# Bias rows repeated from a DRAM row, forget rows loaded behind the first weights, later sums at the second gate tile

## The reference, cut to what matters

```python
def dilated_bias(rel_bias, g):                       # mixer B: one bias row per group and head
    r = B_DILATIONS[g]
    n_slots = B_WINDOWS[g] // r + 1
    b = rel_bias[t5_bucket(jnp.arange(n_slots, dtype=jnp.int32) * r)]
    return b[:, g * B_HPG:(g + 1) * B_HPG].T.astype(jnp.float32)
...
    # mixer A, sample tokens: forget values come by page from a pool, then a cumulated sum
    logf = jnp.concatenate(
        [logf_pool[page_table].reshape(DB, P, H).astype(jnp.float32), logf_new], axis=1)
    cT = jnp.cumsum(logf, axis=1).transpose(0, 2, 1)
    s = jnp.einsum("nqhd,nkhd->nhqk", q, k).astype(jnp.float32) * ATTN_SCALE
    s = s + cT[:, :, P:, None] - cT[:, :, None, :]
...
    h = rmsnorm(x, g_pre)
    qa, ka, va, fa, za, qb, kb, vb, zb, ga, gb = jnp.split(h @ w_in, cuts, axis=-1)
    u_a = (o_a.reshape(N, L, A_WIDTH) * jax.nn.silu(za)) @ w_br_a
    u_b = (o_b.reshape(N, L, B_OUT_WIDTH) * jax.nn.silu(zb)) @ w_br_b
    x = x + rmsnorm((sigmoid(ga) * u_a + sigmoid(gb) * u_b) @ w_out, g_post)
```

## Time and profile before

| | |
|---|---|
| runs | 790.59, 792.75, 792.93 us (median 792.75) |
| span of the profiled execution | 790.7 us; no other time of that execution is given |
| PE busy | 650.9 us (82%) |
| DVE, ACT, POOL busy | 358.0, 248.3, 181.0 us |
| chain that ended last | PE 64%, SP's queue 16%, DVE 7%, DMA 4%, POOL 3% |
| SP's queue in that chain | L406 8%, L407 4% |
| DMA queues | q1 71.77 MB, q0 27.68 MB |

### The profile page before, as it was taken

How to read it: one execution, slowest core, us unless ns; L and a number is a source line. 1 busy time by engine, 2 the same in 40 slices (tenths; PEclk the granted TensorE clock), 3 DMA queues, 4 the chain that set the end, 5 groups by cost and what they waited for, 6 DMA issues and landing times.

```text
span 790.7 us, 12686 instructions
## 1 busy us (share of the span) xinstructions
PE 650.9 (82%) x4740; PEld 590.3 (75%) x4740; DVE 358.0 (45%) x759; ACT 248.3 (31%) x539; POOL 181.0 (23%) x203
## 2 busy tenths in 40 slices
PE   3940009999999999999998977899999989847892
PEld 3730009999899889999998977876548989837892
DVE  1820004555555544344446777432215743194662
ACT  5520012443443433343331222321112323464410
POOL 2610033011010003000034778301101221366000
PEclk9885559999999999999999999999999999987997
DMA  7199978652461433822316998735552321123111
GB/s 213 9 28 27 28 140 268 217 187 79 141 206 42 154 87 90 313 80 80 108 28 200 295 317 269 205 111 156 151 162 88 107 81 47 34 80 107 41 41 55
DMA packets 106219, 100.26 MB, mean 127 GB/s; under 512 B 6591, under 2 KB 93927, under 8 KB 105872
## 3 DMA queue, kind: packets, MB, share of 16 engines
q1 hardware_dynamic: 101936, 71.77, 31.6%
q0 software_dynamic: 4176, 27.68, 16.9%
q10 hardware_dynamic: 48, 0.01, 0.0%
HBM read 90.31 MB, written 27.96 MB: 150 GB/s over the span
## 4 chain that ended last, share of the span: by engine, by line
PE 64%; SPq 16%; DVE 7%; issue 4%; DMA 4%; POOL 3%; ACT 2%; POOLq 0%; DVEq 0%; ACTq 0%
PE pj L790 43%; SPq L406 8%; PE tr L782 4%; SPq L407 4%; PE pv L740 4%; PE pv L926 3%; DMA kv_b<-in_cache_b_kv_dram 2%; PE sc L893 2%; PE sc L901 2%; PE pv L744 2%; DVE yT L1687 1%; PE sc L790 1%; POOL prod L623 1%; PE sc L898 1%; SPq L395 1%
## 5 line engine op out<-in xcount | busy, mean ns | idle before, releaser
L790 PE MATMUL pj<-h_hi,w_hi 128*128 128x260 f32 x1088 | 323.9, 298 | 101.8 <-DVE w_lo L1315 78.6
L790 PE MATMUL pj<-h_lo,w_hi 128*128 128x260 f32 x1088 | 313.6, 288 | 0.0
L790 PE MATMUL pj<-h_hi,w_lo 128*128 128x260 f32 x1088 | 313.4, 288 | 0.0
L790 PEld LDWEIGHTS pj<-h_hi,w_hi 128*128 128x128 f32 x1088 | 211.6, 194 | 117.8 <-DVE w_lo L1315 79.0
L790 PEld LDWEIGHTS pj<-h_lo,w_hi 128*128 128x128 f32 x1088 | 211.7, 195 | 0.0
L790 PEld LDWEIGHTS pj<-h_hi,w_lo 128*128 128x128 f32 x1088 | 211.4, 194 | 0.0
L1315 DVE TENSOR_TENSOR w_lo<-w_raw,w_hi 128x1024 fp32r<-128x1024 f32 (+1 forms) x76 | 93.9, 1240 | 128.7 <-ACT w_hi L1061 128.1
L1061 ACT ACTIVATE w_hi<-w_raw 128x1024 fp32r<-128x1024 f32 (+2 forms) x84 | 81.5, 972 | 166.8 <-DMA w_raw<-in_w_in_dram 106.6
L1322 DVE COPY probT<-tr 128x256 f32<-128x256 f32 (+3 forms) x56 | 27.3, 488 | 52.9 <-PE tr L782 52.9
L623 POOL TENSOR_TENSOR prod<-kv_a,qbc 128x512 f32<-128x512 f32 x24 | 32.6, 1385 | 19.2 <-DMA kv_b<-in_cache_b_kv_dram 14.4
L926 PE MATMUL pv<-v_tok,probT 128*128 128x64 f32 x216 | 29.4, 263 | 0.0
(11 more groups left out here) (326 smaller groups left out, 961.1 us busy)
## 6 DMA issues: line engine op xcount, KB each, us to landing
w_raw<-in_w_in_dram SPq DMA_DIRECT2D x52, 512.0 KB, 5.0
kv_a<-in_cache_a_kv_dram SPq DMA_DIRECT2D x64, 256.0 KB, 3.5
out_dram<-in_cache_b_kv_dram POOLq DMA_DIRECT2D x16, 1022.0 KB, 10.0
qbc<-q_dram SPq DMA_DIRECT2D x8, 640.0 KB, 5.6
kv_b<-in_cache_b_kv_dram SPq DMA_DIRECT2D x32, 128.0 KB, 3.0
w_raw<-in_w_out_dram SPq DMA_DIRECT2D x8, 512.0 KB, 3.9
w_raw<-in_w_ple_gate_dram SPq DMA_DIRECT2D x8, 512.0 KB, 4.4
x_in<-in_x_prompt_dram SPq DMA_DIRECT2D x4, 512.0 KB, 6.5
```

What stands on the lines that cost most here:

```text
L790: ins = nc.tensor.matmul(out, w[:, k0, :], x[:, c_x, lo:hi], start=first and i == 0, stop=last and i == 2)
```

## The change

The diff has three parts.

1. **Bias rows.** `gen` goes once into a small DRAM tensor `gen_dram` (three DMAs). The 128 copies of each row are then read from that DRAM row (`bias_copies`, source of step 0) instead of from a partition of SBUF. POOL issues these 12 copies at the head of round 1, behind the stores of the forget values, and the 12 reads into `toep` (`bias_tiles`) at the head of round 2, ahead of round 2's window copies.
2. **Forget rows.** SP loads w3, w4 and w5 first. The 32 rows come eight at a time, behind the other loads of rounds 0 to 3 in SP's list. The wait for the page table stays ahead of the wait for `cum`.
3. **Later sums.** The transposes of `lf_rows` and the four products move from round 0 to behind gate tile 31 (t = 1), into a bank `tr` instead of `pv`; DVE copies `lfT` out at t = 1 and `later` at t = 2. Round 1's wait for `s_lsum` is gone; the addition of `later` waits for its copy.

The diff, cut to its core (left out: the list of semaphore names and three lines of counting):

```diff
@@ -288,6 +288,7 @@
 
         c_dram = nc.dram_tensor("c_dram", [2, AH, SEQ], F32).ap()
         toep_dram = [nc.dram_tensor(f"toep_dram{g}", [BH, P * PITCH[g]], F32).ap() for g in range(BG)]
+        gen_dram = [nc.dram_tensor(f"gen_dram{g}", [BH, PITCH[g]], F32).ap() for g in range(BG)]
         o0_dram = nc.dram_tensor("o0_dram", [SEQ, BO], F32).ap()
         m0_dram, l0_dram = (nc.dram_tensor(n, [SEQ, BH], F32).ap() for n in ("m0_dram", "l0_dram"))
         q_dram = nc.dram_tensor("q_dram", [DEC, ROUNDS * P], F32).ap()
...
@@ -401,12 +404,16 @@
             sp.dma_start(wf_raw[:, :, :], w_in[:, :, COL_F:COL_F + AH]).then_inc(s_wf, 16)
             for n in range(RING):
                 load(n)
-            sp.wait_ge(s_pt, 16)
-            for i in range(DEC * PAGES):
-                page = sp.value_load(pt[0:1, i:i + 1], min_val=0, max_val=POOL_PAGES - 1)
-                sp.dma_start(lf_rows[i:i + 1, :], A["cache_a_logf"][0, bass.ds(page, 1), :, :].rearrange("o t h -> o (t h)")).then_inc(S["s_lfr"], 16)
             for n in range(RING, 2 * RING):
                 load(n)
+
+            def forget_rows(i0, i1):
+
+                for i in range(i0, i1):
+                    page = sp.value_load(pt[0:1, i:i + 1], min_val=0, max_val=POOL_PAGES - 1)
+                    sp.dma_start(lf_rows[i:i + 1, :], A["cache_a_logf"][0, bass.ds(page, 1), :, :].rearrange("o t h -> o (t h)")).then_inc(S["s_lfr"], 16)
+
+            sp.wait_ge(s_pt, 16)
             sp.wait_ge(S["s_cum"], 2)
             sp.dma_start(c_dram[0], cum[:, :]).then_inc(s_cd, 16)
             sp.dma_start(c_dram[1], ncum[:, :]).then_inc(s_cd, 16)
@@ -423,6 +430,7 @@
                 sp.dma_start(k_aug[s][HD:HD + 1, :, 0:SEQ], c_dram[1:2, 2 * r:2 * r + 2, :]).then_inc(s_crow[s], 16)
                 if r:
                     load(3 * r + 5)
+                forget_rows(8 * r, 8 * r + 8)
             with sp.Fori(ROUNDS_A + 1, ROUNDS) as r:
                 for j, col in enumerate((COL_QB, COL_KB, COL_VB)):
                     sp.wait_ge(s_lo, 3 * r + j - RING + 1)
@@ -531,14 +539,23 @@
 
             pool.wait_ge(S["s_gen"], BG)
             for g in range(BG):
-                for h in range(BH):
-                    src = gen[g][h:h + 1, :].unsqueeze(1).to_broadcast([1, P, PITCH[g]])
-                    pool.dma_start(toep_dram[g][h:h + 1, :].rearrange("o (i y) -> o i y", i=P), src).then_inc(S["s_gend"], 16)
-            pool.wait_ge(S["s_gend"], 16 * BG * BH)
-            for g in range(BG):
-                for h in range(BH):
-                    rows = toep_dram[g][h, P - 1:P - 1 + P * (PITCH[g] - 1)].rearrange("(i y) -> i y", i=P)
-                    pool.dma_start(toep[g][:, h, :], rows[:, 0:TOEP[g]]).then_inc(S["s_toep"], 16)
+                pool.dma_start(gen_dram[g], gen[g][:, :]).then_inc(S["s_gend"], 16)
+
+            def bias_copies():
+
+                pool.wait_ge(S["s_gend"], 16 * BG)
+                for g in range(BG):
+                    for h in range(BH):
+                        src = gen_dram[g][h:h + 1, :].to_broadcast([P, PITCH[g]])
+                        pool.dma_start(toep_dram[g][h, :].rearrange("(i y) -> i y", i=P), src).then_inc(S["s_gent2"], 16)
+
+            def bias_tiles():
+
+                pool.wait_ge(S["s_gent2"], 16 * BG * BH)
+                for g in range(BG):
+                    for h in range(BH):
+                        rows = toep_dram[g][h, P - 1:P - 1 + P * (PITCH[g] - 1)].rearrange("(i y) -> i y", i=P)
+                        pool.dma_start(toep[g][:, h, :], rows[:, 0:TOEP[g]]).then_inc(S["s_toep"], 16)
 
             pool.wait_ge(s_used, USE_LOGF + 1)
             pool.dma_start(alf_p[0, 0].rearrange("(b p) h -> p b h", p=P), lf_small[:, 0:NB, :]).then_inc(S["s_lfst"], 16)
@@ -547,6 +564,10 @@
 
             for r in range(1, ROUNDS + 1):
                 t = r - 1
+                if r == 1:
+                    bias_copies()
+                if r == 2:
+                    bias_tiles()
                 if r <= ROUNDS - 1:
 
                     for g in range(BG):
@@ -699,11 +720,12 @@
             pe.wait_ge(s_used, USE_LF + 1)
             cols = lfT[:, :, :, :].rearrange("p g s h -> p (g s h)")
             c0, c1 = EARLY_COLS["later"]
-            nc.tensor.matmul(pv[0][:, 0:256], early[:, c0:c1], cols, start=True, stop=False)
+            b = tr[USE_LSUM % 2]
+            nc.tensor.matmul(b[:, 0:256], early[:, c0:c1], cols, start=True, stop=False)
             for k in range(1, PAGES):
                 w = 256 - 64 * k
-                last = nc.tensor.matmul(pv[0][:, 0:w], ones, cols[:, 64 * k:256], start=False, stop=k == PAGES - 1)
-            last.then_inc(S["s_suf"], 1)
+                last = nc.tensor.matmul(b[:, 0:w], ones, cols[:, 64 * k:256], start=False, stop=k == PAGES - 1)
+            return last
 
         def sample_rows_t(pe, turn):
 
@@ -950,13 +972,9 @@
                         for k in range(NB):
                             nc.tensor.transpose(b[:, k * AH:(k + 1) * AH], logf[:, k * P:(k + 1) * P], ident[0:AH, 0:AH])
                         use.up(nc.tensor.transpose(b[0:DEC, NB * AH:(NB + 1) * AH], logf[:, SEQ:T], ident[0:AH, 0:AH]))
-                    if r == 0 and i == 10:
-                        later_sums_t(pe, turn)
                     if 1 <= i <= nu:
                         probs_t(r, i - 1)
                     if 2 <= i <= nu + 1:
-                        if r == 1 and i == 2:
-                            pe.wait_ge(S["s_lsum"], 1)
                         values(r, i - 2)
                     if i == 10 and r and is_a(r):
                         pe.wait_ge(s_pve, unit0[r] + 8)
@@ -975,6 +993,8 @@
                 for k in range(4):
                     project(n, k)
                 t = n - TILE_G - 3
+                if t == 1:
+                    use.up(later_sums_t(pe, turn))
                 if t == 10:
                     sample_rows_t(pe, turn)
                 if t == 12:
@@ -1507,10 +1527,6 @@
                         b = tr[used.n % 2]
                         V.tensor_copy(lf_small[:, 0:NB, :].rearrange("p b h -> p (b h)"), b[:, 0:NB * AH])
                         used.up(V.tensor_copy(lf_small[0:DEC, NB, :], b[0:DEC, NB * AH:(NB + 1) * AH]))
-                    if r == 0 and i == 10:
-                        out_of_turn((lfT[:, :, :, :].rearrange("p g s h -> p h s g"), lambda b: b[:, 0:256].rearrange("p (h s g) -> p h s g", h=AH, g=PAGES)))
-                        dve.wait_ge(S["s_suf"], 1)
-                        V.tensor_copy(later[:, :], pv[0][:, 0:PAGES * DEC * AH]).then_inc(S["s_lsum"], 1)
                     if 1 <= i <= nu:
                         probs_out(r, i - 1)
                     if i % 4 == 3:
@@ -1608,6 +1624,10 @@
                 if n >= TILE_Z:
                     silu(n)
                 lo_part(n + RING)
+                if t == 1:
+                    out_of_turn((lfT[:, :, :, :].rearrange("p g s h -> p h s g"), lambda b: b[:, 0:256].rearrange("p (h s g) -> p h s g", h=AH, g=PAGES)))
+                if t == 2:
+                    out_of_turn((later[:, :], lambda b: b[:, 0:PAGES * DEC * AH]))
                 if n >= TILE_Z:
 
                     i = n - TILE_Z
@@ -1620,6 +1640,7 @@
                     sample_logits(t)
                 if t == DEC - 1:
                     dve.wait_ge(S["s_red"], 6 * DEC)
+                    dve.wait_ge(s_used, USE_LSUM + 1)
                     la = lg_a[:, :, :, :].rearrange("p g s h -> p (g s h)")
                     V.tensor_tensor(la, la, later[:, :], ALU.add).then_inc(S["s_lga"], 1)
                 if t == 10:
```

More of the change, by code:

```diff
@@ L344, in units @@
             return [(hd, qb) for qb in range(NB) for hd in range(2)] if r <= ROUNDS_A + 2 else [(0, None), (1, None)]
-        USE_LOGF, USE_LF = DC // 2, DC // 2 + 1
-        unit0, use0, u, k = {}, {}, 0, DC // 2 + 2
+        USE_LOGF = DC // 2
+        unit0, use0, u, k = {}, {}, 0, DC // 2 + 1
         for r in range(1, ROUNDS + 1):
@@ L352, in build @@
         UNITS, USE_SAMP, USE_COMBINE = u, k, k + 8
-        USE_ROW = USE_COMBINE + 2
+        USE_LF = USE_COMBINE + 2
+        USE_LSUM = USE_LF + 1
+        USE_ROW = USE_LF + 2
         pt_use = {unit0[r] + i: use0[r] + 2 + i for r in unit0 for i in range(len(units(r)))}
@@ L370, in build @@
         s_p = sem("s_p")
-        names = ("s_relb s_gt s_gv s_ssz s_sqx s_nv s_y0 s_rs s_rsb s_hraw s_hh s_hl s_hlv s_wfhi s_wflo s_gen s_gent s_gend s_toep "
+        names = ("s_relb s_gt s_gv s_ssz s_sqx s_nv s_y0 s_rs s_rsb s_hraw s_hh s_hl s_hlv s_wfhi s_wflo s_gen s_gent s_gend s_gent2 s_toep "
                  "s_biasm s_bias s_fm s_fx s_fe s_fu s_fl s_logf s_cum s_clear s_xst s_xsv s_xo s_xoe s_copy s_ge s_g3 "
                  "s_o0 s_o0r s_md s_wexp s_cw s_comb s_selfp s_sst s_qd s_qb0 s_qb1 s_kp0 s_kp1 s_bk0 s_bk1 s_prod s_prodv s_red s_pz "
-                 "s_lfr s_suf s_lsum s_lga s_selfr s_nma s_nmb s_exa s_exb s_pn s_dm s_dv s_ds s_samp s_os s_osm s_ot s_ov s_slfd "
```

(1 more changed line is left out.)

## The result

The changed kernel takes 741.01 us in the median of four runs (738.38 to 742.90); the kernel before, on the same chip, 792.0 us in the median of four. The ratio is 0.936, with a 95% interval from 0.933 to 0.9389. The forecast was 747 us, with a range from 719 to 764. The profiled execution took 739.46 us, its span is 737.2 us, so 2.26 us lie around the span, where the forecast put 2.05. In the tables of this document the medians and ranges count every run, while ratios and their intervals leave out one slow run each of three kernels (735.79, 745.23 and 749.50 us), so a ratio is not always the quotient of two medians.

What follows compares the result with a forecast made beforehand. PE's standstill behind w1, from forget rows ahead of weights and slow bias copies, was taken as the bound. Span 790.7 - 72.3 + 25 (hold) + 1.5 (restart) + 0.5 (later sums) = 745.4; with 2.05 around it, 747 us, range 719 to 764.

Steps and rivals of the forecast that it cites:

- The standstill: PE's stall behind w1 goes, as weights precede forget rows and slow bias copies move: round 1 starts 72.3 us earlier.
- The hold: Round 1: w6 and w7 wait in DMA queues beside 4 MB of window copies; 25 us taken, 14 to 28 forecast.
- cold restart: PE restarts cold behind the hold: 24 matmuls take 4.47 us against 2.95, costing 1.5 us.
- upper end: Case of the hold: w6 lands at 93 to 94, ACT has waited 27 us, and round 1 stands with it.
- only w7 is caught: Case of the hold: w6 slips through whole and ACT waits only for w7, 14 us.
- middle case: Case of the hold: w6 lands at about 87 between window copies, ACT waits 20 us, then finds w7 there.
- The sign of the hold: ACT's longest wait in the profile is for w6, from about 67 to 93; round 2 begins near 116.
- The later sums: At gate tile 31 PE falls some 7 us behind, mostly hidden by its waits for ACT: 0.5 us, between 0 and 7.
- Edits at little: Edits costed at little: bias copies from DRAM take 6.4 to 16 us; later forget rows delay loads up to 9.9 us.
- The full gain: Rival: w6 and w7 both get through before the long window copies; 721 us, or up to 724; 19 in 100.
- The longer hold: Rival: bias copies take 16 us and push window copies back by 9; hold 35 us, time 757; 13 in 100.
- the slower outcome: Rival: bias copies from DRAM stay slow at 69.5 us, w6 waits 89 us; 812 us; 3 in 100.

Runs made afterwards that it cites:

- rows and sums alone: The changed kernel with the bias copies of the kernel before (parts 2 and 3 without part 1): 801.70 us, ratio 1.012 to the kernel before.
- The repeat: The changed kernel once more, unchanged, on another chip: 743.19 us, ratio 0.9358 to the kernel before.
- The third execution: The changed kernel with the later sums split, transposes behind gate tile 31, products behind tile 32, `later` copied at t = 3: 735.59 us.
- early and late copies: The changed kernel with round 1's window copies issued at about 12 us (724.87 us), or in round 9 instead (726.55 us).
- the rows a round later: The changed kernel with the forget rows one round later in SP's list: 730.67 us, ratio 0.9186 to the kernel before.
- the one of all three: The changed kernel with round 1's window copies early, forget rows a round later and later sums in two steps: 718.20 us, ratio 0.9069.

## Why the prediction was right

**The standstill.** Forecast 72.3 us, measured 72.07. Round 1's first transposes were put at 58.5 and came at 58.75. Of the two causes that it named, the bias copies are the one without which nothing is won (the rows and sums alone are slower than before); the rows' place in SP's list, with the later sums out of round 0, is worth 13.8 us at this point, which round 1 then takes back.

**The hold.** This is the step that was mis-sized: 25 us and 1.5 for the cold restart were taken, 18.2 us measured in all. The mechanism held: the runs with the window copies moved away lose the hold, and w7 landed at 95.4, when the queues ran dry, which the prediction put at 93 to 94. What failed is the choice of the value, near the upper end "since w8 is the nearest row". w8 had been issued six us behind the first copy; w6 was issued 2.6 us ahead of it (the prediction had 62 and 62.8), and got through in 8.9 us. Its case for that, "only w7 is caught", was worked out as 93.5 - 79.6 = 14, and ACT's wait for w7 is 14.3. The repeat is its middle case: w6 landed at 84.5 (there 87), ACT waited 16.9 us (there 20) and found w7 ready at 100.06 (there 99.6). The third execution, with 12.8 us of waits, is a little below both. So the point belonged with those two cases, not near the upper end.

Of its signs, PE has no long gap from 50 to 58, SP issues w3 at 34.59 and is through with the eighth row at 60.36. The sign of the hold came otherwise: ACT's longest wait for a weight in rounds 1 to 10 is for w7, and round 2 begins at 107.50 and not near 116.

**The later sums.** Forecast 0.5 us, in a range from 0 to 7; measured 3.5 us up to the addition and 2.1 to the end of the samples' stage. PE's delay is as forecast: 4.2 us of waiting and 2.6 of products (384.34 to 386.94) against some 7. The cover was there in part: behind it PE stands 5.0 us waiting for ACT (396 to 443 us), where it stood 9.7. What was left out is that ACT's next `w_hi` hangs on PE, and DVE's `w_lo` on that (4.82 us), and DVE is what the samples' stage runs on.

**Edits at little.** The bias copies from a DRAM row were through 13.7 us behind the first issue (56.81 to 70.5), inside the bounds of 6.4 and 16. The eight rows behind w8, put at up to 9.9 us, took SP 34.55, so that w9 was issued only at 102.51; ACT didn't wait for it, and the other rows cost no wait of their own that a trace shows.

**The sum.** In spans: -72.07 (start) + 18.16 (round 1) - 1.67 (rounds 2 to 10) + 3.55 and - 1.47 (samples' stage up to the addition, and all behind it) = -53.5, which is 790.7 - 737.2. The forecast was 745.4, 8.2 too long; 8.3 of that is the hold, 1.7 the rounds behind it, and the later sums and the start make up 1.8 the other way. The 1.67 us lie mainly in one place, where PE was busy without a gap in both: from 388 to 404 us the granted clock was 0.91 and 0.88 (means of 8 us, between the levels of 1.2 and 2.4 GHz) in the profiled execution before, and 1.00 in the same work after (334 to 350). No run shows that as the change's doing: two executions of the changed kernel differ by 1.4 us in these rounds (259.2 and 260.6).

**The rivals.** The full gain would have needed what the early and late copies bring (725 and 727), and that is still above the 721 to 724 forecast. The longer hold and the slower outcome fell with the bias copies landing at 70.5. That slower outcome, weights held behind slow bias copies, is nevertheless real in this kernel: it is what the rows and sums do without the bias part.

What stays open is why w6 gets through in 8.9 us in one execution and takes 16.1 or 23.7 in others with the same order of issue, while w7 takes 34 to 35 in each.

## What to carry to other kernels

When a load is moved earlier or later, look at what large transfer is issued within a few us of its new place, on any queue, and what slack the load has there; a hold by a burst of copies goes to the next load in line unless the burst itself moves to a stretch where nobody waits for a load. A start just ahead of the burst is not enough: w7 set out 2.2 us ahead of it and was caught in all three executions, w6 set out 2.6 us ahead and took anything from 8.9 to 23.7 us, and with 9 us or more ahead the two took 4.3 and 3.7. Where several cases of a hold are worked out and none is excluded, take a value between them and not that of the one nearest row. When two causes stand behind one stall, taking away one alone can be worth nothing, or the whole.

## What the runs showed of the hardware

SP's issue itself gets slow while window copies and weights move: eight forget rows took 34.55 us from 67.92 on, against 9.01 for the eight before them, and a single issue of `q_aug` took 17.52 us in the run with the rows a round later and 0.61 in the one of all three, where round 1's window copies are gone from there. The traces show this as time of the issue and not as a wait, and the list of forget rows holds no wait; everything behind it in SP's list is late too.

128 readings of each of 12 rows cost by where the rows lie: from one partition the 12 copies took 69.5 us (35.71 to 105.2), from a DRAM row 13.7 (56.81 to 70.5), single ones 3.6 to 7.7 us from issue to landing, the later ones beside w6's and w7's loads. The copies from one partition hold up what runs beside them: w5 took 67.7 us in the run of rows and sums alone.
